# A seven-part change to the order of work in a one-core decoder-layer kernel: early input splits for the output GEMM, alternated squares, paired additions, earlier spreads, new cross-attention lanes

## The chip, the cores and the metric

One core of a Trainium2 chip runs the whole kernel. The metric is the device time of one execution in microseconds (us); lower is better. TensorE is called PE below, VectorE DVE, ScalarE ACT, GpSimd POOL and SyncE SP, as in the profile.

## The reference

One layer of a hybrid decoder, in float32, for a prompt of 512 tokens and a sample group of 8 x 4 tokens that share the weights (544 tokens in all, model width 1024):

```python
xn = rms_norm(x, lp['n_mix_pre'])
(m_qkv, s_z, s_xbc, s_dt, h_q, h_f, h_i, h_g, g_qkv, g_z, g_b, g_a) = split_cols(xn @ w_in, IN_SIZES)
# four mixers: block-sparse attention, Mamba-2 scan (ssm), HGRN2, gated DeltaNet (gdn)
# x = x + rms_norm(concat(o_a, o_b, o_c, o_d) @ w_out)
def memory_kv(mem, norm_w, w_kv):
    k, v = jnp.split(rms_norm(mem, norm_w) @ w_kv, 2, axis=-1)
def memory_cross_attention(xn, w_q, k, v, w_o):
    q = (xn @ w_q).reshape(b, L, X_HEADS, X_DH)
    s = jnp.einsum('blhd,bmhd->bhlm', q, k) * X_DH ** -0.5
    p = jax.nn.softmax(s, axis=-1)
    o = jnp.einsum('bhlm,bmhd->blhd', p, v)
    return o.reshape(b, L, X_HEADS * X_DH) @ w_o
def swiglu(xn, w_gu, w_down):
    g, u = jnp.split(xn @ w_gu, 2, axis=-1)
    return (jax.nn.silu(g) * u) @ w_down
```

Each of the three blocks has an RMS norm ahead of it and one behind it, and adds its result to x. Outputs are the new x, the new keys and values, the memory's keys and values, and the states.

## The kernel before

**Numbers and tiles.** Activations lie transposed, 128 channels on the partitions and 544 tokens along a row, as 8 tiles (KD = 8). Every large GEMM is done as three products: both operands are split into a high part in a short format and the rest as a low part, and PE adds high x high, high x low and low x high (`mm3`, `tile_mm`). A tile of 544 tokens is two halves of 272 (HT), each in its own PSUM bank, so one input tile k and one block of 128 output channels cost 6 matmuls of 272 columns. ACT makes the high part of a weight chunk (L239, `split_hi`) and POOL its low part (L248, `split_lo`); three chunks are in flight. The high parts of the inputs are made by ACT (`part_hi`, L743), the low ones by DVE (`part_lo`, a subtraction through `tt`, L706).

**Order.** Each engine has its program written out by hand; semaphores join them. A stage is a piece of each engine's program (`stage`). Where `enter` is true, an engine waits at its start until PE, DVE and ACT have all ended the stage before. Inside some stages several generators are interleaved by a string of letters, one letter for one step up to its next `yield`: `LANES` for the ssm stage ("m" the mixers, "p" the paged sample attention), `GDN_LANES` for the tail of the gated DeltaNet ("t") and the memory GEMM ("k"), `CX_LANES` for the cross stage ("p" prompt, "s" sample). All engines follow the same string.

**The ssm stage.** Two "p" steps come first (the sample's own scores, and the transposes of the first key tile into a bank), then the first "m" step: `spread_tensor` spreads two rows of per-head numbers over 128 partitions, four matmuls of 272 columns. DVE needs them for the inputs of the scan (`ssm_xdt`).

**The memory GEMM and the tail of gdn.** `mem_tensor` multiplies the memory with its 16 weight chunks, one "k" step each, then transposes the keys in four more steps. ACT splits a chunk in each step and copies two results in every second (L3112, L3119). Between them run the five token tiles of the gdn tail; the last step of a tile copies its outputs to OM tiles 6 and 7 (L3002), and its state update on DVE (two L706 additions and products ahead of that copy) is what PE needs for the next tile.

**The output GEMM (stage wout).** Its inputs are the 8 tiles of OM: 0 and 1 from attention, 2 and 3 from ssm, 4 and 5 from HGRN2, 6 and 7 from gdn. `wout_start_*` starts it: DVE squares tiles 6 and 7, PE sums the squares over heads (`sums`, matmuls with blk64, banks 6 and 7), ACT makes the roots (L976, L978), and DVE scales the tiles with them. Meanwhile PE does the products of tiles 0 to 5 for the first three output blocks (LAST = 3), then those of tiles 6 and 7. The first block's `gemm_mm` is what frees its weight slot.

**The norm transitions.** After the output GEMMs of the mixers (run 0) and of the cross attention (run 1), the sum over channels, the root, the residual and the next norm have to be done before the next GEMM's results can be scaled. It is done in two halves of tokens. DVE's `x_vector` makes the scaled tile (L936), the residual (L706) and the low part (L926) of each tile; ACT makes the high part (`x_hi_scalar`, L882) and the square (`x_square_scalar`, L886). PE starts the next GEMM on these parts (`next_start_tensor`). `pre_sum_vector` then adds the squares of the 8 tiles on DVE, PE sums them over partitions (`pre_sum_tensor`), ACT makes the root (L877, L878), and only then PE goes on.

**The cross stage.** A prompt step does the scores of one (head, token tile) pair on PE, the row maximum on DVE (L3191), the exponential on ACT (L3220), the scaling on DVE (L3197), the transposes on PE, and now and then a product with the values (pv). A sample step transposes one pair of memory key tiles and does one score; the first of these scores waits for queries that POOL pads (L3563 to L3569). Behind 16 sample scores come the sample softmax and eight products with values, whose loads go through four slots.

## Time and profile before

| | |
|---|---|
| median of 3 runs | 1240.22 us |
| lowest, highest | 1240.07, 1244.26 us |
| profiled execution: its own time | 1239.63 us |
| profiled execution: span | 1238.0 us |
| mean granted clock of TensorE | 0.969 |
| busy: PE, DVE, ACT, POOL | 94%, 48%, 36%, 36% |

The span is from the first to the last instruction; the time of an execution has some 1.6 us more around it. Busy shares are means over all stages. The granted clock is a share of 2.4 GHz; 0.50 is 1.2 GHz.

### The profile page before, as it was taken

How to read it: one execution, taken by the hardware profiler on the slowest of the kernel's cores; microseconds unless marked ns; L12 is line 12 of the kernel's file. 1: busy time of each engine (PE TensorE's matmuls, PEld its weight loads, DVE VectorE, ACT ScalarE, POOL GpSimd, SP SyncE). 2: the span in 40 equal slices, each digit the busy share in tenths (PEclk: the TensorE clock that was granted, in tenths of full speed). 3: DMA queues.
4: the chain of work that ended last, by engine and by line, in shares of the span. 5: the costliest groups of instructions: out<-in, count | busy, mean ns of one | idle time of the engine just before them, and what ended most of it. 6: DMA issues, size and time to landing. Idle time of an engine off the chain costs nothing.

```text
span 1238.0 us, 24845 instructions
## 1 busy us (share of the span) xinstructions
PE 1166.6 (94%) x10272; PEld 1014.0 (82%) x10272; DVE 598.7 (48%) x1068; ACT 448.9 (36%) x802; POOL 441.0 (36%) x370
## 2 busy tenths in 40 slices
PE   7999999988988988998989899999999999999998
PEld 6999997855655688887989656988999999977775
DVE  5699735236478886413291463184433334321003
ACT  6323234245544444233552342454222223221212
POOL 8433533053417121452603200614434444433331
PEclk9999999989979998898998899999999999999999
DMA  6332523066659422336414753312222232232221
GB/s 161 91 86 69 175 74 121 2 202 183 192 156 329 134 80 81 104 107 211 120 35 141 235 174 115 104 51 86 86 86 87 85 100 82 75 103 71 83 85 72
DMA packets 176581, 143.45 MB, mean 116 GB/s; under 512 B 15955, under 2 KB 162820, under 8 KB 176214
## 3 DMA queue, kind: packets, MB, share of 16 engines
q1 hardware_dynamic: 166838, 120.44, 32.5%
q0 software_dynamic: 7200, 20.23, 5.4%
q8 instruction: 81, 1.33, 0.5%
q10 hardware_dynamic: 2432, 1.21, 0.3%
q14 instruction: 30, 0.25, 0.1%
HBM read 131.64 MB, written 10.20 MB: 115 GB/s over the span
## 4 chain that ended last, share of the span: by engine, by line
PE 74%; DVE 12%; issue 4%; ACT 4%; POOL 2%; DMA 1%; SPq 1%; POOLq 0%; DVEq 0%; ACTq 0%
PE PS L264 67%; PE PS L267 7%; DVE SC L706 2%; DVE PROJ L1939 2%; POOL W_LO L248 2%; DVE XN L936 1%; DVE XT L706 1%; DVE PROJ L2358 1%; SPq L536 1%; DVE XN L706 1%; DVE XN_parts L926 1%; ACT PROJ L1342 1%; DVE PROJ L706 1%; ACT W_HI L239 0%; DVE PROJ L1940 0%
## 5 line engine op out<-in xcount | busy, mean ns | idle before, releaser
L248 POOL TENSOR_TENSOR W_LO<-W,W_HI 128x1024 fp32r<-128x1024 f32 x128 | 313.8, 2456 | 635.1 <-ACT W_HI L239 634.9
L264 PE MATMUL PS<-XN_parts,W_HI 128*128 128x272 f32 x1184 | 340.6, 288 | 0.0
L264 PE MATMUL PS<-OM_parts,W_HI 128*128 128x272 f32 x960 | 277.3, 289 | 0.0
L264 PEld LDWEIGHTS PS<-XN_parts,W_HI 128*128 128x128 f32 x1184 | 223.2, 188 | 0.0
L239 ACT ACTIVATE W_HI<-W 128x1024 fp32r<-128x1024 f32 x128 | 134.2, 1054 | 209.5 <-PE PS L264 209.5
L264 PE MATMUL PS<-OM_parts,W_LO 128*128 128x272 f32 x704 | 203.9, 290 | 0.0
L264 PE MATMUL PS<-SC_parts,W_HI 128*128 128x272 f32 x608 | 179.9, 296 | 3.9 <-POOL W_LO L248 3.2
L264 PEld LDWEIGHTS PS<-OM_parts,W_HI 128*128 128x128 f32 x960 | 181.8, 189 | 0.1
L264 PE MATMUL PS<-SC_parts,W_LO 128*128 128x272 f32 x608 | 176.8, 291 | 0.0
L264 PEld LDWEIGHTS PS<-OM_parts,W_LO 128*128 128x128 f32 x704 | 132.3, 188 | 0.0
L264 PEld LDWEIGHTS PS<-SC_parts,W_HI 128*128 128x128 f32 x608 | 115.6, 190 | 8.3 <-issue 6.1
L264 PEld LDWEIGHTS PS<-SC_parts,W_LO 128*128 128x128 f32 x608 | 115.4, 190 | 0.0
L264 PE MATMUL PS<-W_HI,PROJ_parts 128*128 128x512 f32 (+1 forms) x320 | 110.6, 374 | 0.0
L264 PE MATMUL PS<-W_HI,SC_parts 128*128 128x256 f32 (+1 forms) x288 | 87.3, 337 | 0.0
L264 PEld LDWEIGHTS PS<-W_HI,PROJ_parts 128*128 128x128 f32 x320 | 60.9, 190 | 13.3 <-issue 2.8
L706 DVE TENSOR_TENSOR SC<-SC 128x272 f32<-128x272 f32 (+6 forms) x68 | 37.2, 550 | 50.3 <-ACT SC L866 41.1
L264 PE MATMUL PS<-OM_parts,PROJ_parts 128*128 128x272 f32 x256 | 54.7, 303 | 5.9 <-DVE XN_parts L926 3.7
L264 PEld LDWEIGHTS PS<-W_HI,SC_parts 128*128 128x128 f32 x288 | 53.1, 197 | 8.4 <-issue 4.1
L264 PE MATMUL PS<-W_LO,SC_parts 128*128 128x512 f32 (+1 forms) x160 | 58.4, 365 | 0.0
L706 DVE TENSOR_TENSOR SC<-PS,RSQ 128x544 f32<-128x544 f32 x22 | 15.9, 724 | 87.1 <-PE PS L264 85.2
L3410 ACT ACTIVATE SC<-SC 128x544 f32<-128x544 f32 x22 | 14.5, 658 | 114.9 <-DVE SC L706 114.9
L1342 ACT ACTIVATE PROJ<-PS 128x512 f32<-128x512 f32 x68 | 40.1, 598 | 40.3 <-PE PS L267 40.3
(405 smaller groups left out, 2073.7 us busy)
## 6 DMA issues: line engine op xcount, KB each, us to landing
W<-in_w_gu SPq DMA_DIRECT2D x44, 512.0 KB, 3.9
W<-in_w_in SPq DMA_DIRECT2D x30, 512.0 KB, 3.8
W<-in_w_down SPq DMA_DIRECT2D x22, 512.0 KB, 3.7
W<-in_w_xkv SPq DMA_DIRECT2D x16, 512.0 KB, 3.7
W_scratch<-in_cache_moba_v SPq DMA_DIRECT2D x36, 128.0 KB, 4.8
W_scratch<-in_cache_moba_v POOLq DMA_DIRECT2D x36, 128.0 KB, 4.9
XT<-in_cache_moba_k SPq DMA_DIRECT2D x32, 128.0 KB, 2.8
XT<-in_cache_moba_k POOLq DMA_DIRECT2D x32, 128.0 KB, 2.4
```

What stands on the lines that cost most here:

```text
L239: nc.scalar.activation(hi_lo(n)[0], raw_chunk(n), ACT.Copy)\
L248: nc.gpsimd.tensor_tensor(hi_lo(n)[1], raw_chunk(n), hi_lo(n)[0].bitcast(F32), ALU.subtract).then_inc(S("weights_split"), 1)
L264: return nc.tensor.matmul(out, lhsT, rhs, start=start, stop=stop, skip_group_check=True)
L267: return nc.tensor.transpose(out, in_, ident[0:k, 0:k])
L536: sp.dma_start(dst, src).then_inc(S(name), 16)
L706: return V.tensor_tensor(out, x, y, op)
L926: V.scalar_tensor_tensor(lo(k)[:, TOKENS[run][j]], XT[:, k, TOKENS[run][j]], par(GAINS[run][1] + k), hi(k)[:, TOKENS[run][j]].bitcast(F32) ...
L936: last = V.scalar_tensor_tensor(xn[:, k, c_], xn[:, k, c_], par(GAINS[run][0] + k), rsq[:, c_], ALU.mult, ALU.mult)
L1342: return A.activation(o_, i_, ACT.Copy)
L1939: V.scalar_tensor_tensor(dst[:, d:SEQ], src[:, 0:SEQ - d], wt[3 - d], dst[:, d:SEQ], ALU.mult, ALU.add)
L2358: V.copy_predicated(h_store(i, w), level.bitcast(I32), src).then_inc(S("h_lv_out"), 1)
L3410: A.activation(f_g[:, t % 2, :], f_g[:, t % 2, :], ACT.Silu).then_inc(S("ff_silu"), 1)
```

## The change

Seven edits.

1. `ssm_start_tensor`: PE does the two spreads ahead of the lanes of the ssm stage.
2. `early_hi_scalar`, `early_lo_vector`: OM tiles 2, 3, 4, 0 and 1 are split during the memory GEMM, in ACT's "k" steps 10 to 14 and DVE's steps 11 to 15. Only tiles 5, 6 and 7 are split in stage wout.
3. `wout_start_tensor`: PE does the products of the five early tiles for block 0, then the first head sums, the five tiles of block 1, the second sums, block 2, then tile 5 and tiles 6 and 7 for all three blocks.
4. PE and DVE no longer wait at the entry of stage wout. In its place PE waits for the last copy of the gdn tail (`tail_vn_out`), and for the last copies of the memory's keys.
5. `y_gemm_scalar`: ACT makes a high part of the second half and then a square of the first half, tile by tile, and the squares of the second half at the end. Before it made all squares of the first half, then high part and square of the second half in turn.
6. `pre_sum_vector`: the squares of two tiles are added to two others at once (three additions of 2 x 272), then the two sums to each other.
7. `CX_LANES`: six prompt steps come right behind the first sample step; fewer are left at the end.

```diff
@@ -909,9 +909,9 @@
             for k in range(6, KD):
                 x_hi_scalar(s, run, 0, k)
             for k in range(KD):
+                x_hi_scalar(s, run, 1, k)
                 x_square_scalar(run, 0, k)
             for k in range(KD):
-                x_hi_scalar(s, run, 1, k)
                 x_square_scalar(run, 1, k)
             root_half_scalar(s, run, 3, 0)
             root_half_scalar(s, run, 4, 1)
@@ -942,32 +942,45 @@
             x_lo_vector(v, run, j, KD - 1)
+        EARLY = (2, 3, 4, 0, 1)
+
+        def early_hi_scalar(s, x):
+            s.wait_ge(*((S("states_made"), 3) if x < 3 else (S("tail_tok"), 5 + NT)))
+            A.activation(sc_hi[:, EARLY[x], :], OM[:, EARLY[x], :], ACT.Copy).then_inc(S("part_hi"), 1)
+
+        def early_lo_vector(v, x):
+            k = EARLY[x]
+            v.wait_ge(S("part_hi"), IN_BEFORE["wout"] + x + 1)
+            tt(OM_R[:, k, :], OM[:, k, :], sc_hi[:, k, :].bitcast(F32), ALU.subtract).then_inc(S("part_lo"), 1)
+
         def wout_start_tensor(pe):
             def sums(k):
                 for j in range(2):
                     last = mm(bank(6 + j)[:, 0:HT], blk64, half(g_qg[:, k, :], j), True, True)
                 last.then_inc(S("tail_sum"), 1)
+            def products(i, ks):
+                wh, wl = weights(pe, first["wout"] + i)
+                for k in ks:
+                    if i == 0:
+                        pe.wait_ge(S("part_lo"), IN_BEFORE["wout"] + (EARLY.index(k) if k in EARLY else k) + 1)
+                    for j in range(2):
+                        last = tile_mm(pe, half_bank("wout", i, j), "wout", wh, wl, TOKENS[0][j], [k], 0, EARLY[0], KD - 1)
+                return last
+
+            pe.wait_ge(S("tail_vn_out"), NT + 1)
+            products(0, EARLY)
+            pe.wait_ge(S("kvm_out"), 20)
             pe.wait_ge(S("tail_sq"), 3)
             sums(0)
+            products(1, EARLY)
+            pe.wait_ge(S("tail_root"), 6)
+            sums(1)
+            products(2, EARLY)
             for i in range(LAST):
-                wh, wl = weights(pe, first["wout"] + i)
-                for k in range(6):
-                    if i == 0:
-                        pe.wait_ge(S("part_lo"), IN_BEFORE["wout"] + k + 1)
-                    for j in range(2):
-                        tile_mm(pe, half_bank("wout", i, j), "wout", wh, wl, TOKENS[0][j], [k], 0, 0, KD - 1)
-                if i == 0:
-                    pe.wait_ge(S("tail_root"), 6)
-                    sums(1)
+                products(i, [5])
             for i in range(LAST):
-                wh, wl = weights(pe, first["wout"] + i)
-                for k in range(6, KD):
-                    if i == 0:
-                        pe.wait_ge(S("part_lo"), IN_BEFORE["wout"] + k + 1)
-                    for j in range(2):
-                        last = tile_mm(pe, half_bank("wout", i, j), "wout", wh, wl, TOKENS[0][j], [k], 0, 0, KD - 1)
-                last.then_inc(S("gemm_mm"), 1)
+                products(i, range(6, KD)).then_inc(S("gemm_mm"), 1)
             pe.wait_ge(S("tail_root"), 8)
         def wout_start_scalar(s):
@@ -977,11 +990,8 @@
                 s.wait_ge(S("tail_root"), 6 + 2 * k)
                 A.activation(g_qg[:, k, :], g_qg[:, k, :], ACT.Exp, scale=-0.5).then_inc(S("tail_root"), 1)
-            for k in range(3):
-                part_hi(s, "wout", k)
+            part_hi(s, "wout", 5)
             root(0)
-            for k in range(3, 6):
-                part_hi(s, "wout", k)
             root(1)
             for k in range(6, KD):
                 s.wait_ge(S("normed"), KD + k - 5)
@@ -994,8 +1004,7 @@
             v.wait_ge(S("tail_sq"), 3)
             for c_ in range(2):
                 link(V.scalar_tensor_tensor(Y[:, c_, :], Y[:, c_, :], par(R_GNORM), proj[:, C_GZ + c_, :], ALU.mult, ALU.mult))
-            for k in range(6):
-                part_lo(v, "wout", k)
+            part_lo(v, "wout", 5)
             for c_ in range(2):
                 v.wait_ge(S("tail_root"), 7 + 2 * c_)
                 tt(Y[:, c_, :], Y[:, c_, :], g_qg[:, c_, :], ALU.mult).then_inc(S("normed"), 1)
@@ -1032,12 +1041,10 @@
         def pre_sum_vector(v, run):
             for j in range(2):
                 c_ = TOKENS[run][j]
-                for k in range(1, KD):
-                    v.wait_ge(S("norm_sq_s"), 2 * KD * run + KD * j + k + 1)
-                    last = tt(nsq[:, 0, c_], nsq[:, 0, c_], nsq[:, k, c_], ALU.add)
-                    if k < KD - 1:
-                        link(last)
-                last.then_inc(S("pre_acc"), 1)
+                for k in range(2, KD, 2):
+                    v.wait_ge(S("norm_sq_s"), 2 * KD * run + KD * j + k + 2)
+                    link(tt(nsq[:, 0:2, c_], nsq[:, 0:2, c_], nsq[:, k:k + 2, c_], ALU.add))
+                tt(nsq[:, 0, c_], nsq[:, 0, c_], nsq[:, 1, c_], ALU.add).then_inc(S("pre_acc"), 1)
         KH = KF // 2
@@ -1968,6 +1975,11 @@
+        def ssm_start_tensor(pe):
+            pe.wait_ge(S("att_out"), 4)
+            for c_ in range(2):
+                spread_tensor(pe, 2 * c_, 0, c_)
+
         def ssm_tensor(pe):
             def pre(i):
                 t0, w, _ = TILES[i]
@@ -1986,9 +1998,6 @@
                     last = tr(bank(3)[0:w, k * P:(k + 1) * P], src, P)
                 last.then_inc(S("ssm_pre"), 1)
-            pe.wait_ge(S("att_out"), 4)
-            for c_ in range(2):
-                spread_tensor(pe, 2 * c_, 0, c_)
             yield
             pe.wait_ge(S("ssm_xdt"), 1)
             for i, (t0, w, _) in enumerate(TILES):
@@ -2999,7 +3008,12 @@
                 def outputs():
                     v.wait_ge(S("tail_o"), 5 + x + 1)
-                    link(V.tensor_copy(OM[:, 6:8, sl], bank(2)[:, 0:2 * w].rearrange("p (c l) -> p c l", l=w)))
+                    kept = V.tensor_copy(OM[:, 6:8, sl], bank(2)[:, 0:2 * w].rearrange("p (c l) -> p c l", l=w))
+                    if x < NT - 1:
+                        link(kept)
+                    else:
+                        kept.then_inc(S("tail_vn_out"), 1)
+                        v.wait_ge(S("tail_vn_out"), NT + 1)
                 if sample:
                     outputs()
@@ -3100,6 +3114,8 @@
                     gated = OM[:, 4 + step, :]
                     link(V.scalar_tensor_tensor(gated, gated, par(R_HNORM), proj[:, C_HG + step, :], ALU.mult, ALU.mult))
                     tt(gated, gated, h_norm[step], ALU.mult)
+                if 9 <= step < 14:
+                    early_lo_vector(v, step - 9)
                 yield
         def mem_scalar(s):
@@ -3111,6 +3127,8 @@
                         s.wait_ge(S("kvm_mm"), 2 * n + mt + 1)
                         A.activation(mkv[:, mt, n * 256:(n + 1) * 256], bank(MEM_BANKS[mt])[:, 0:256], ACT.Copy,
                                      scale=mem_rs[:, mt:mt + 1]).then_inc(S("kvm_out"), 1)
+                if 10 <= c_ < 15:
+                    early_hi_scalar(s, c_ - 10)
                 yield
             split_hi(s, first["wout"] + NH)
             for q in range(4):
@@ -3136,7 +3154,7 @@
         CX_Q = NPROJ // 2
         PV_STEP = (6, 8, 10, 12, 14, 16, 17, 18)
         CX_STEPS = 21
-        CX_LANES = "psps" * 8 + "psp" * 2 + "pps" + "psp" * 7 + "pspsppp"
+        CX_LANES = "ps" + "pppppp" + "psps" * 7 + "ps" + "psp" * 2 + "pps" + "psp" * 4 + "ps" * 5
         def cross_lanes(prompt, sample):
             steps = {"p": prompt, "s": sample}
@@ -3465,12 +3483,12 @@
         def _(pe):
             stage(pe, "inputs", lambda: inputs_tensor(pe))
             stage(pe, "win", lambda: normed_samples_tensor(pe), lambda: params_tensor(pe), lambda: win_tensor(pe), enter=False)
-            stage(pe, "ssm", lambda: lanes(mixer_lane(pe, ssm_tensor(pe), hgrn_tensor(pe)), moba_sample_tensor(pe), unit_tensor(pe), ssm_norm_tensor(pe)))
+            stage(pe, "ssm", lambda: ssm_start_tensor(pe), lambda: lanes(mixer_lane(pe, ssm_tensor(pe), hgrn_tensor(pe)), moba_sample_tensor(pe), unit_tensor(pe), ssm_norm_tensor(pe)))
             stage(pe, "gdn", lambda: gdn_tensor(pe), lambda: gdn_lanes(gdn_tail_tensor(pe), mem_tensor(pe)), enter=False)
             stage(pe, "wout",
                   lambda: wout_start_tensor(pe),
                   lambda: y_gemm_tensor(pe, "wout", LAST),
-                  lambda: wxq_tensor(pe))
+                  lambda: wxq_tensor(pe), enter=False)
             stage(pe, "cross", lambda: cross_lanes(cross_prompt_tensor(pe), cross_sample_tensor(pe)), enter=False)
             stage(pe, "wxo",
                   lambda: wxo_start_tensor(pe),
@@ -3489,7 +3507,7 @@
             stage(v, "wout",
                   lambda: wout_start_vector(v),
                   lambda: y_gemm_vector(v, "wout"),
-                  lambda: wxq_vector(v))
+                  lambda: wxq_vector(v), enter=False)
             stage(v, "cross", lambda: cross_lanes(cross_prompt_vector(v), cross_sample_vector(v)),
                   lambda: cross_out_vector(v), enter=False)
             stage(v, "wxo",
```

The order of PE's instructions where stage gdn ends and stage wout begins. `SC,XN` is the last product of the gdn tail, `CN,PROJ` the transposes of the memory's keys, `SC,CN` the head sums, and the rows with parts are products of the GEMM. Before:

```order
L264 MATMUL PS<-SC,XN 64x128 x4
L267 MATMUL PS<-CN,PROJ 128x128 x12
L264 MATMUL PS<-SC,CN 128x272 x2
L264 MATMUL PS<-SC_parts,W_HI 128x272
L264 MATMUL PS<-OM_parts,W_HI 128x272
```

With the change:

```order
L264 MATMUL PS<-SC,XN 64x128 x4
L267 MATMUL PS<-CN,PROJ 128x128 x12
L264 MATMUL PS<-SC_parts,W_HI 128x272
L264 MATMUL PS<-OM_parts,W_HI 128x272
L264 MATMUL PS<-SC_parts,W_LO 128x272
```

The sums went from ahead of the first product to behind the thirtieth.

ACT in the first norm transition, from the root of the first norm on (L877, L878). L882 is a high part, L886 a square. Before:

```order
L877 ACTIVATE RSQ<-PS,CN 128x272
L878 ACTIVATE RSQ<-RSQ 128x272
L882 ACTIVATE OM_parts<-XT,SM 128x272 x2
L886 ACTIVATE SC<-XT 128x272 x8
L882 ACTIVATE OM_parts<-XT,SM 128x272
L886 ACTIVATE SC<-XT 128x272
```

With the change:

```order
L877 ACTIVATE RSQ<-PS,CN 128x272
L878 ACTIVATE RSQ<-RSQ 128x272
L882 ACTIVATE OM_parts<-XT,SM 128x272 x3
L886 ACTIVATE SC<-XT 128x272
L882 ACTIVATE OM_parts<-XT,SM 128x272
L886 ACTIVATE SC<-XT 128x272
```

The eight squares in a row are gone from this place; at the end of the transition there are nine in a row instead.

PE at the start of the cross stage. `PROJ 128x256` are the scores of one prompt step, `CN,SC` its transposes, `CN,PROJ ... x8` one sample step's key transposes, `SC,XN` a sample score:

```order
 L264 MATMUL PS<-PROJ 128x256 x2
-L267 MATMUL PS<-CN,PROJ 128x128 x16
+L267 MATMUL PS<-CN,PROJ 128x128 x8
+L264 MATMUL PS<-PROJ 128x256 x2
+L267 MATMUL PS<-CN,SC 128x128 x2
+L264 MATMUL PS<-PROJ 128x256 x2
+L267 MATMUL PS<-CN,SC 128x128 x2
+L264 MATMUL PS<-PROJ 128x256 x2
+L267 MATMUL PS<-CN,SC 128x128 x2
+L267 MATMUL PS<-CN,PROJ 128x128 x8
 L264 MATMUL PS<-SC,XN 32x256 x4
```

Three prompt scores and three transposes now stand between the first sample step and the first sample score, which comes from behind two key tiles as before.

## Rows read from the trace of the kernel before

**Rows 1.** The page: busy time of PE, and the chain that ended last by engine
```profile
PE 1166.6 (94%) x10272; PEld 1014.0 (82%) x10272; DVE 598.7 (48%) x1068; ACT 448.9 (36%) x802; POOL 441.0 (36%) x370
...
PE 74%; DVE 12%; issue 4%; ACT 4%; POOL 2%; DMA 1%; SPq 1%; POOLq 0%; DVEq 0%; ACTq 0%
```

**Rows 2.** Windows of PE: from:to length, busy (instructions), granted clock, DMA share, GB/s
```profile
254.31:264.12 9.81, 9.81 (x49) 0.50 0.91 276
...
565.75:570.29 4.54, 1.71 (x4) 0.79 1.00 241
570.29:575.10 4.81, 4.81 (x21) 0.50 1.02 374
575.10:591.78 16.68, 16.68 (x129) 1.00 0.35 135
...
653.04:657.10 4.06, 4.06 (x18) 0.50 0.01 4
816.00:839.23 23.23, 18.15 (x132) 1.00 0.00 1
...
693.59:698.00 4.41, 4.41 (x20) 0.50 1.13 316
```

**Rows 3.** Timeline, ssm start: start, length, engine, instruction [idle before <- releaser]; last row the chain
```profile
253.24 0.60 PE L264 MATMUL PS<-SC 128*128 128x32 f32 x4 [3.41 <-DVE W L1688]
256.25 1.11 ACT L2291 ACTIVATE W<-W 128x1088 f32<-128x1088 f32 x1
260.79 0.66 PE L264 MATMUL PS<-PROJ,W 128*32 128x128 f32 x8
...
254.31 3.87 PE PS L264 x8
```

**Rows 4.** Timeline of PE where stage wout begins
```profile
565.09 0.66 PE L267 MATMUL PS<-CN,PROJ 128*128 128x128 f32 x4 [0.25 <-ACT PROJ L3119]
...
567.89 1.71 PE L264 MATMUL PS<-SC,CN 128*128 128x272 f32 x4 [2.14 <-DVE SC L706]
570.29 0.57 PE L264 MATMUL PS<-SC_parts,W_HI 128*128 128x272 f32 x1 [0.69 <-DVE OM_parts L706]
```

**Rows 5.** Groups of 566 to 592: the input parts (xcount, busy us, mean ns)
```profile
L743 ACT ACTIVATE SC_parts<-OM 128x544 fp32r<-128x544 f32 x8 | 4.8, 646 | 0.4 <-DVE OM L706 0.2
L706 DVE TENSOR_TENSOR OM_parts<-OM,SC_parts 128x544 fp32r<-128x544 f32 x8 | 5.4, 720 | 0.3 <-ACT SC_parts L743 0.2
```

**Rows 6.** Timeline of the memory GEMM, and of DVE at 592
```profile
548.75 0.66 DVE L706 TENSOR_TENSOR XN<-XN,SM 128x128 f32<-128x128 f32 x1 [0.55 <-PE PS L264]
552.84 0.47 ACT L3112 ACTIVATE PROJ<-PS,SM 128x256 f32<-128x256 f32 x1 [0.96 <-PE PS L264]
...
592.00 4.81 DVE L706 TENSOR_TENSOR SC<-SC 128x544 f32<-128x544 f32 x2 [10.18 <-ACT SC L866]
```

**Rows 7.** Timeline of the first norm transition, and one double addition at 607
```profile
607.14 0.73 DVE L706 TENSOR_TENSOR SC<-SC 128x544 f32<-128x544 f32 x1 [5.33 <-ACT SC L866]
...
635.26 0.50 DVE L926 SCALAR_TENSOR_TENSOR XN_parts<-XT,SM,OM_parts 128x272 fp32r<-128x272 f32 x1 [0.70 <-ACT OM_parts L882]
644.17 6.50 DVE L706 TENSOR_TENSOR SC<-SC 128x272 f32<-128x272 f32 x14
650.73 1.28 PE L264 MATMUL PS<-SC,CN 128*128 128x272 f32 x2 [1.74 <-DVE SC L706]
653.04 0.60 PE L264 MATMUL PS<-OM_parts,PROJ_parts 128*128 128x272 f32 x1 [1.04 <-ACT RSQ L878]
```

**Rows 8.** Timeline of the cross stage
```profile
688.28 2.49 DVE L3197 TENSOR_SCALAR SC<-SC 128x256 f32<-128x256 f32 x1
693.59 0.66 PE L264 MATMUL PS<-SC,XN 128*32 128x256 f32 x4 [5.30 <-POOL XN L3569]
734.68 0.35 DVE L3197 TENSOR_SCALAR SC<-SC 128x256 f32<-128x256 f32 x1
735.09 0.44 PE L267 MATMUL PS<-CN,SC 128*128 128x128 f32 x2 [0.97 <-DVE SC L3197]
```

## The prediction

> **What bounds the kernel now.** I read the chain of waits first. TensorE (PE) is 94% of the span busy and holds 74% of the chain, DVE 12% [rows 1]: nearly everything that counts is either PE working or PE waiting for one short chain elsewhere. So a change can win only where PE stands still, or where it works at the low clock. The windows view shows the second kind [rows 2]: at a granted clock of 0.50, that is 1.2 of 2.4 GHz, PE worked for 9.81 us after 254.31, 4.81 us after 570.29, 4.06 us after 653.04 and 4.41 us after 693.59. Each of these follows a stretch in which PE stood still or nearly so; 816.00 to 839.23 has as much idle time (5.1 us of 23.2) at a clock of 1.00, so whether a gap is followed by the low level differs from gap to gap. The four stretches come to 23.1 us, of which half is lost. The diff touches just those places: the ssm start, the start of the output GEMM, both norm transitions, and the start of the cross stage. Outside them the order of work is the same, and there PE is dense: I assume that what is won passes through to the end.
>
> **Part 1, the ssm start.** PE waits 3.41 us for DVE before 253.24 [rows 3], and right behind, from 254.31, runs the four spread matmuls for 3.87 us at the low level. Now the spreads come first. They need only the stage entry (about 250.8) and the attention outputs, so at 2.4 GHz they take about 1.9 us and end by 252.8, inside the idle stretch. What is late next is ScalarE: it copies the second key transpose only after a table load and the activation that ends at 257.36 [rows 3]; with a 0.6 us copy the second score can start at 258.0 where it started at 260.79. That is 2.8 us. If PE is also at 2.4 GHz there, the next 3.3 us of work take half, and it is 4.6 us. PE now idles some 2 us at 256, so I take 3.4 us, between the two; from below the bound is 0, if a wait further on in this stage swallows it.
>
> **Part 2, the start of the output GEMM.** Before, PE ends the memory transposes at 565.75, waits 2.14 us for the squares that DVE starts after the stage barrier, does the head sums, waits 0.69 us for the first low part, and starts the products at 570.29 [rows 4], the first 4.81 us of them at 0.50 [rows 2]. Now five of eight tiles are split beforehand, DVE does not wait for the barrier, and PE starts products of those five at once: at 566.0, counting 0.25 us for the last drain. Idle time won: 2.14 + 0.69 - 0.25 = 2.6 us. The low clock: PE has no gap any more between 565.75 and 570.29, so I expect the 6.1 us of work between 568.3 and 575.1 at full rate, 3.0 us. Sum 5.6 us. Nothing is late next: 30 products at 0.125 us (16.68 us for 129 instructions, sums among them [rows 2]) take 3.8 us, so the first sums run at 569.8, the second at 574.4; the roots, the gating of tiles 6 and 7 and their two parts (0.65 and 0.72 us a tile [rows 5]) are done by 579, and PE asks for tile 6 at 581. The last 36 products, during which the next weights are made, keep their order, so the 1.7 us wait for those weights stays. Bounds: 2.6 us if the clock falls anyway, 5.9 us if the drain costs nothing.
>
> The five splits themselves lie on ScalarE and DVE during the memory GEMM, where both idle. Ten instructions of 0.65 or 0.72 us; two of ScalarE's delay a weight split by 0.6 us; PE waited for no weights between 500 and 590, so there is cover. One place is tight: ScalarE makes the fourth high part after its copy at 552.84 [rows 6], so at 553.95; DVE stands waiting for it with the state update behind it that before ran at 548.75, and PE asks for that state at 555.60. 553.95 + 0.72 + 0.66 + 0.29, with gaps, is 555.7: about 0.1 us late. The row that speaks against it: two DVE additions of the same size took 4.81 us together, 2.4 each, at 592.00 [rows 6] while POOL made low parts of weights. If the fourth split takes 2.4 us, PE waits 1.8 us. In the Trainium skill, GPSIMD Engine Reference, Key points, POOL shares its SBUF interfaces with DVE, and contention is stated for DVE instructions with two SBUF inputs; these splits are of that kind. By that rule the sum would be 1.8 us smaller. The trace agrees at 592.00; I keep 0.1 because before POOL's next W_LO starts at 554.33, and the ScalarE split ahead of it moves back 0.65 us, behind most of this one.
>
> **Part 3, the two norm transitions.** ScalarE did eight squares of the first half in one run before the second half's first high part, and DVE waited 0.70 us for that part (635.26 [rows 7]). With high part and square alternating, ScalarE needs 0.9 us a tile and DVE 1.3 us, so high parts come as soon as the residual is there: 0.70 us won. Then the 14 additions took 6.50 us. Now they are 6 of double width at 0.73 us plus a semaphore gap (607.14 [rows 7]) and 2 single ones at 0.46: 6 x 0.77 + 2 x 0.46 = 5.5 us, 1.0 us less. The last square of the second half is ready at 646.0, before it is needed. The sum of the second half is ready 1.7 us earlier, PE's sum at 650.73 moves with it, and so does the restart at 653.04, behind two ScalarE instructions. The second transition has the same rows (14 additions in 6.50 us, the same waits). 2 x 1.7 = 3.4 us. That the clock does not fall at the first would add 2.4 us (0.56 of the 1.28 us sum, half of 4.06 us less the drop's end); that it falls at the second, where it did not before, would take as much away. I put this at nothing.
>
> **Part 4, the cross stage.** Three more prompt steps come ahead of the first sample score, which waits 5.30 us for POOL's padded queries [rows 8]. They fill part of the gap, not all: the first of them needs DVE's scaling, which is held until 690.77 beside POOL's work (2.49 us against 0.35 elsewhere), so PE still idles about 2.4 us from 688.3. From there PE does four scores and three transposes where it did one and two key tiles, but at 1.20 GHz if the clock falls as before at 691.4: about as much time lost as won. At the other end fewer prompt steps are left to cover the sample softmax; the wait of 0.97 us at 735.09 [rows 8] becomes one of 1 to 2 us. Net 0, between -2 us (clock low and longer waits) and +2.5 us (clock stays up).
>
> **Sum.** 3.4 + 5.6 + 3.4 + 0 = 12.4 us off the profiled execution's 1239.6 us: 1227.2 us. The median of the three runs is 0.6 us above that execution, so I predict 1227.8 us.
>
> **Rivals.**
> The clock does not come back. Gaps remain everywhere (2 us at 256, 1.3 us before the second norm sum, 2.4 us at 688). Then parts 1 and 2 give 2.8 and 2.6, part 3 gives 3.4 and part 4 takes 2: 6.8 us, 1233.4 us. For it: the low level came after four of five such gaps. Against: behind 565.75 no gap is left. In the Trainium skill, TensorE: Matmul & The Clock Gate, Part 1, the default state is throttled and activity releases it; the rows agree, and do not say how much idle time is enough. Chance 0.18.
> The ssm start is absorbed and the cross stage loses. The 3 us go into waits for ScalarE's copies or the page loads between 258 and 350, and part 4 costs 2 us: 5.6 + 3.4 - 2 = 7.0 us, 1233.2 us. For it: ScalarE, not PE, ends the waits of that stage. Against: they are few. Chance 0.15.
> POOL stretches the early splits as priced above: 1.8 us less, 1229.6 us. Chance 0.04.
> Slower than before: the low clock spreads. The cross stage now begins with PE waiting on DVE and ScalarE at every step, and the GDN tail has one wait more. A low stretch costs half its length, 2.0 us (653.04) to 4.9 us (254.31). From six short or three long new ones on, the 12.4 us are gone; with eight short ones, 16 us, it is 1243.8 us. Against it: total idle time falls. Chance 0.03.
> The forecast has the remaining 0.60.
>
> **How the numbers follow.** All good ends together (4.6, 5.9, 5.8 and 2.5) give 18.8 us, 1221.4 us; the two middle rivals lie at 1233, and with a little more lost at 1236. Range 1220 to 1236. A measurement of this kernel tells about 0.5%, 6.2 us, from no change: faster means under 1234.0. The forecast lies there nearly whole, the rivals at 1233 a little over half: faster 0.82, same 0.15, slower 0.03.
>
> **What would show it.** Right: the four spread matmuls before PE's wait at the ssm start, and the second score 3 to 4 us earlier; less than 0.5 us between the last memory transpose and the first product, at a clock of 1.00; 14 additions replaced by 8 in 5.5 us; restarts of both transitions 1.7 us earlier relative to their GEMM; the cross stage as long as before. Wrong: a PE wait over 1 us in the GDN tail for DVE's state, a wait for tile 6 at the output GEMM, a span of the ssm stage that does not shrink, or a cross stage longer by more than 2 us.

## The result, and the profile after

The changed kernel took 1226.6 us (median of 4 executions, 1225.0 to 1230.0), against 1240.6 us for the kernel before on the same chip (median of 4, 1240.1 to 1244.3): a ratio of 0.988, with a 95% interval of 0.985 to 0.991. That is 14 us faster; 1227.8 us was forecast, with a range of 1220 to 1236. The profiled execution took 1227.1 us at a span of 1225.5 us, 12.5 us below the profiled span of before.

The page of the changed kernel, busy times and chain by engine:

```profile
PE 1159.9 (95%) x10272; PEld 1008.6 (82%) x10272; DVE 597.9 (49%) x1056; ACT 448.6 (37%) x802; POOL 441.8 (36%) x370
...
PE 74%; DVE 13%; issue 4%; ACT 3%; POOL 2%; DMA 1%; SPq 1%; POOLq 0%; DVEq 0%; ACTq 0%
```

Nothing of the picture has changed against [rows 1]: PE bounds it. PE's busy time is 6.7 us lower with the same 10272 instructions, and the mean granted clock is 0.976 where it was 0.969. I read those 6.7 us as work that ran at 2.4 GHz where it ran at 1.2, and the rest as idle time; the table below, stretch by stretch, has 8.5 us less of low clock, part of which PE sat through idle. The same windows of PE as in [rows 2], at their new places (from:to length, busy (instructions), granted clock, DMA share, GB/s):

```profile
254.22:264.00 9.78, 8.67 (x83) 0.83 0.89 269
366.09:370.65 4.56, 4.56 (x36) 0.63 0.88 255
402.66:408.75 6.09, 6.09 (x102) 0.56 0.78 256
564.02:568.00 3.98, 3.98 (x31) 1.00 1.01 247
568.00:584.23 16.23, 16.23 (x123) 1.00 0.69 254
642.82:647.22 4.40, 4.40 (x23) 0.61 0.02 4
826.71:831.00 4.29, 4.29 (x34) 1.00 0.00 0
677.77:680.42 2.65, 0.00 (x2) 1.00 0.81 249
680.42:684.77 4.35, 4.35 (x16) 0.61 1.15 308
```

The start of the output GEMM (564.02) is at full clock now. The ssm start is mostly so. Behind the first transition (642.82) and at the cross start (680.42) a low stretch is still there, though shorter. And there are two low stretches where before had none or a shorter one, at 366 and at 403.

The ssm start and the start of stage wout on PE, which answer to [rows 3, 4]:

```profile
251.31 2.10 PE L264 MATMUL PS<-OM,CN 4*128 4x272 f32 x8 [0.87 <-DVEq L3463]
253.75 0.63 PE L264 MATMUL PS<-SC 128*128 128x32 f32 x4 [0.35 <-DVE W L1695]
...
258.68 0.42 PE L264 MATMUL PS<-PROJ,W 128*32 128x128 f32 x8 [1.11 <-ACT PROJ L1349]
...
563.10 0.66 PE L267 MATMUL PS<-CN,PROJ 128*128 128x128 f32 x4 [0.25 <-ACT PROJ L3137]
564.02 0.36 PE L264 MATMUL PS<-SC_parts,W_HI 128*128 128x272 f32 x1 [0.26 <-issue]
...
567.88 1.08 PE L264 MATMUL PS<-SC,CN 128*128 128x272 f32 x4
```

The spreads (8 records, 2.10 us) fill the wait of 3.41 us down to 0.35. At 564.02 the first product follows the last transposes after 0.26 us, and the sums at 567.88 wait for nothing.

Both transitions, DVE and PE, which answer to [rows 7]:

```profile
635.66 5.34 DVE L706 TENSOR_TENSOR SC<-SC 128x544 f32<-128x544 f32 x8
638.43 0.73 PE L264 MATMUL PS<-SC,CN 128*128 128x272 f32 x2 [0.22 <-DVE SC L706]
641.06 0.73 PE L264 MATMUL PS<-SC,CN 128*128 128x272 f32 x2 [1.15 <-DVE SC L706]
642.82 0.40 PE L264 MATMUL PS<-OM_parts,PROJ_parts 128*128 128x272 f32 x1 [1.04 <-ACT RSQ L878]
...
824.95 0.72 PE L264 MATMUL PS<-SC,CN 128*128 128x272 f32 x2 [1.15 <-DVE SC L706]
826.71 0.39 PE L264 MATMUL PS<-OM_parts,PROJ_parts 128*128 128x272 f32 x1 [1.04 <-ACT RSQ L878]
```

Eight additions take 5.34 us where fourteen took 6.50, and PE's wait for the last sum is 1.15 us where it was 1.74.

**Where the 12.5 us went.** The same instruction was looked up in both traces at the borders of each stretch, and the difference of the starts taken. "Low" is what the clock costs in it: one minus the granted clock, summed over the stretch in pieces of 0.25 us of the windows view, in us. Where PE stands still during a low piece it costs less than that.

| stretch of PE, by the start in the trace of before | before, us (low) | after, us (low) |
|---|---|---|
| ssm start, 248.91 to 264.76 | 15.85 (5.1) | 11.49 (1.7) |
| mixers, first part, 264.76 to 369.03 | 104.27 (10.2) | 104.15 (10.2) |
| mixers, second part, to 444.49 | 75.46 (3.4) | 78.73 (6.8) |
| gdn to 519.91 | 75.42 (6.8) | 74.04 (5.1) |
| gdn tail and memory GEMM to 563.75 | 43.84 (0) | 43.83 (0) |
| start of the output GEMM to 591.49 | 27.74 (3.4) | 22.18 (0) |
| output GEMM to 626.60 | 35.11 (0) | 34.94 (0) |
| first transition to 653.04 | 26.44 (1.5) | 23.94 (0) |
| its restart to 657.84 | 4.80 (1.9) | 4.52 (1.7) |
| cross, first part, 671.04 to 700.03 | 28.99 (3.4) | 29.33 (1.7) |
| cross, second part, to 761.24 | 61.21 (0) | 61.04 (0) |
| second transition, 799.97 to 839.58 | 39.61 (0) | 37.41 (0) |

Beside these only the start of the program moved (0.6 us later, a load). The gain of 4.4 us at the ssm start is paid back by 3.3 us in the second part of the mixers, and there the low column accounts for all of it (3.4 us).

### The profile page after: what moved, and what is told of

Its sections match the earlier page's. It is cut to its first block, busy times and chain, and to the rows that moved or that the text cites. A ratio compares the mean times of both kernels' runs of the same rounds, so it can differ in the third digit from the quotient of the medians.

```text
span 1225.5 us, 24818 instructions
## 1 busy us (share of the span) xinstructions
PE 1159.9 (95%) x10272; PEld 1008.6 (82%) x10272; DVE 597.9 (49%) x1056; ACT 448.6 (37%) x802; POOL 441.8 (36%) x370
## 4 chain that ended last, share of the span: by engine, by line
PE 74%; DVE 13%; issue 4%; ACT 3%; POOL 2%; DMA 1%; SPq 1%; POOLq 0%; DVEq 0%; ACTq 0%
PE PS L264 67%; PE PS L267 7%; DVE SC L706 2%; DVE PROJ L1946 1%; POOL W_LO L248 1%; DVE XN L936 1%; DVE XT L706 1%; DVE PROJ L2367 1%; SPq L536 1%; DVE XN L706 1%; DVE XN_parts L926 1%; ACT PROJ L1349 1%; DVE PROJ L1947 1%; DMA XN<-in_cache_mem_v 1%; DVE PROJ L706 1%
## 5 line engine op out<-in xcount | busy, mean ns | idle before, releaser
L706 DVE TENSOR_TENSOR SC<-SC 128x544 f32<-128x544 f32 (+7 forms) x56 | 35.3, 633 | 46.9 <-ACT SC L866 38.0
```

The source lines that it names most:

```text
L706: return V.tensor_tensor(out, x, y, op)
```

## The experiments

Twelve kernels ran, in four groups; in each group the kernel before ran beside them. Ratios are to it, with their 95% interval. Executions of one kernel scatter by 3 to 14 us, so a ratio resolves some 3 us, and the stretches of the trace are what tells the parts apart.

| kernel | median, us | ratio to before |
|---|---|---|
| edit 1 alone | 1239.7 | 0.998 (0.996 to 1.001) |
| edits 2, 3, 4 alone | 1235.3 | 0.995 (0.992 to 0.997) |
| edits 5, 6 alone | 1235.4 | 0.995 (0.993 to 0.997) |
| edit 7 alone | 1242.3 | 1.000 (0.998 to 1.002) |
| the changed kernel again | 1226.1 | 0.990 (0.987 to 0.993) |
| changed, old lanes | 1228.8 | 0.991 (0.988 to 0.994) |
| changed, sums first | 1230.7 | 0.991 (0.988 to 0.994) |
| changed, sums repeated | 1227.3 | 0.989 (0.986 to 0.991) |
| changed, zero fills late | 1226.7 | 0.988 (0.985 to 0.991) |
| changed, sums first, entry waits | 1230.0 | 0.990 (0.989 to 0.992) |
| edit 6 alone | 1237.7 | 0.996 (0.994 to 0.997) |
| changed, fills late and sums repeated | 1224.5 | 0.986 (0.983 to 0.989) |

Kernel before in the four groups: 1241.8, 1241.9, 1242.6 and 1241.5 us. The four parts alone give -2.1, -6.5, -6.3 and +0.6 us by their medians, -14.3 in all, as the whole change does (-14.0); each of the four is known to some 3 us only, so the close agreement is luck.

**The ssm start alone.** The kernel before, with edit 1:

```diff
+            pe.wait_ge(S("att_out"), 4)
+            for c_ in range(2):
+                spread_tensor(pe, 2 * c_, 0, c_)
...
-            pe.wait_ge(S("att_out"), 4)
-            for c_ in range(2):
-                spread_tensor(pe, 2 * c_, 0, c_)
             yield
```

> The kernel before with edit 1 alone (the spreads ahead of the lanes of the ssm stage). The forecast's step gives 3.4 us. In the changed kernel the shift of PE was 4.4 us behind the ssm start, but only some 2.6 us of it were left at 520. Theory A (the gain is real at its place, and further on it is eaten by low stretches of PE at 367 to 371 and 401 to 409, which come with the new timing): 2.0 to 4.4 us faster, the second score near 258.1 to 258.7, and whatever is missing behind 300 is in longer low stretches. Theory B (a wait for DVE or ACT between 270 and 480 swallows it): under 1 us faster, with new or longer waits in the mixers, and the low stretches as before.

The ssm start took 13.77 us with 5.1 of low, against 15.85 us with the same 5.1 before: 2.1 us. Behind it nothing was lost (104.28, 75.47 and 75.47 us with the same low as before). Timeline of PE, and the window over it:

```profile
249.91 2.51 PE L264 MATMUL PS<-OM,CN 4*128 4x272 f32 x8 [0.87 <-DVEq L3447]
252.35 1.06 PE L264 MATMUL PS<-SC 128*128 128x32 f32 x4
...
257.91 0.65 PE L264 MATMUL PS<-PROJ,W 128*32 128x128 f32 x8 [1.11 <-ACT PROJ L1342]
```

```profile
252.35:261.89 9.54, 8.43 (x53) 0.51 0.87 276
```

The order is as in the changed kernel, but here PE is at 1.2 GHz until 261.89. So theory A holds at its lower end, by the trace; the ratio of the medians (0.996 to 1.001) can't be told from no change. The edit itself is worth 2.1 us, and the other 2.3 us of the changed kernel's 4.4 are a clock that was up.

**The start of the output GEMM alone.** The kernel before, with edits 2 to 4 (their diff stands above).

> The kernel before with edits 2, 3 and 4 alone (early splits, new order of the output GEMM's start, no entry wait). Theory A (idle time won 2.6 us and a low stretch of 6.1 us of work at full rate, 3.0 us): 5.6 us faster, no row at a clock of 0.50 between 563 and 590, and PE reaches the last product of the first three blocks 5.6 us earlier than before. Theory B (part of the 5.6 us seen there in the changed kernel comes from the shifted time at which it arrives, that is, from edit 1): 2.6 to 4 us faster, with a low stretch behind 566 again.

The stretch took 22.17 us with no low time, 5.6 us less than before. Theory A. It was 22.17 or 22.18 us in all seven profiles with these edits, and with the old start 27.74, 27.70, 27.73 and 27.69 us with 3.4 of low (the kernel before, and with edit 1, edits 5 and 6, edit 7 alone) and 27.07 us with 1.7 (edit 6 alone). Of the five low stretches this is the only one that goes with the edit each time.

**Both transitions alone**, edits 5 and 6; and **edit 6 alone**.

> The kernel before with edits 5 and 6 alone (squares alternated with high parts, additions in pairs). Forecast: 1.7 us at each transition, 3.4 us in all. The changed kernel showed 2.5 and 2.0 us, 4.5 in all. Theory A (1.7 us of waits each time; the rest of the first transition is a low stretch at 643 that happened to be shorter): 3.4 to 4.5 us faster. Theory B (PE loses at the second transition, where the clock stays up before, one low stretch): 1 to 2 us faster with a granted clock of 0.50 behind the second restart.

> The kernel before with edit 6 alone (additions in pairs). Theory A (additions and alternation each win their own wait, as the kernel with both showed 1.95 us at each transition: 0.8 at the residuals, 1.17 at the sums): each transition 1.1 to 1.2 us shorter by unchanged clock, about 2.3 us in all, and DVE's wait of 0.70 us for the second half's first high part still there. Theory B (the pairs only help because the alternation brings the squares in time): under 0.5 us at each transition, and a new wait of DVE for ACT's squares.

With both, the first transition took 23.94 us. Of the kernels that keep the old code, those without low time in it took 25.88 and 25.89: 1.95 us won. The second: 37.41 against 39.39 and 39.34, 1.95 us again, and 2.2 against the 39.61 of the kernel before, which has no low time there either. With the pairs alone they took 24.73 and 38.63 us: 1.15 us won at the first, 0.75 at the second, with 0.4 of low in it. DVE in the first transition with the pairs alone:

```profile
637.67 0.50 DVE L926 SCALAR_TENSOR_TENSOR XN_parts<-XT,SM,OM_parts 128x272 fp32r<-128x272 f32 x1 [0.70 <-ACT OM_parts L882]
...
646.58 4.11 DVE L706 TENSOR_TENSOR SC<-SC 128x544 f32<-128x544 f32 x6
```

The wait of 0.70 us is still there, as theory A of the second text says, and the additions run through. So the pairs give 1.15 and the alternation 0.8 us. In the kernel with both, a low stretch came up behind the second restart and cost 1.7 us, as theory B of the first text has it; the kernel with edit 7 alone, which keeps the old transitions, has one there too, of 2.7 us. The won waits are theory A's; the clock sits on top of them, with or without the edit. The median was 6.3 us lower (3.6 to 8.6 by the interval of the ratio), more than either theory said; the interval holds theory A's 3.4 to 4.5 us in part and excludes theory B's 1 to 2.

**The cross lanes alone, and the changed kernel with the old ones.**

> The kernel before with edit 7 alone (the new lanes of the cross stage). Theory A (what is won in front of the first sample score is lost in the waits at the other end): between 0.5 us faster and 0.5 us slower, with a wait of PE near 688 of 2 to 3 us in place of 5.30, and waits of 1.5 to 2.6 us for the sample softmax. Theory B (the new lanes are worth something by themselves, and in the changed kernel the clock took it away): 1.5 us faster or more. Theory C (they cost, and the clock hid it): 1.5 us slower or more.

> The changed kernel with the old CX_LANES. Theory A (edit 7 is worth nothing, 0.2 us in the trace of the kernel with edit 7 alone): within 1 us of the changed kernel, the cross stage as long as before (from the restart of the first transition to the start of the cross output GEMM). Theory B (the lanes gain once the stage comes earlier): 2 us slower than the changed kernel. Theory C (they cost): 1.5 us faster than it.

The first part of the cross stage took 29.39 us (1.7 low) with the new lanes alone, 29.26 (3.4 low) in the changed kernel with the old ones; over all kernels the new lanes gave 29.33 to 29.56 with 1.7 of low, the old ones 28.78 to 29.26 with 3.4. So they do halve the low stretch each time. It is worth less than 1.7 us: in the kernel before PE stood idle in 2.4 of its 6.8 us (691.2 to 693.6), so it cost 2.2 us, and 1.7 with the new lanes. Against that PE's idle time in both parts together went from 6.4 to 7.2 us in the changed kernel. The second part is about as long (61.0 to 61.4 us, 61.9 once, against 61.2). Theory A: worth nothing, or 0.2 to 0.5 us on the wrong side. The medians (1242.3 against 1241.8, 1226.1 against 1228.8) go either way. The second pair, 2.7 us apart, is what theory B of the second text named, but the intervals of the two kernels overlap, and no stretch of the cross stage shows it.

**The changed kernel again.**

> The changed kernel itself, again, so that the next three kernels have it beside them, and to see how far its executions scatter and with what. Theory A (executions of one kernel differ by how much of the span PE works at the low clock): the times follow the mean granted clock, some 0.9 to 1.0 us for each 0.001 of it, as in the 33 runs of the kernel before (1235.7 to 1249.4 us). Theory B: they scatter with no relation to it. In either case a median of 1225 to 1230 us.

Theory A. Of six executions four had a mean granted clock of 0.975 or 0.976 and took 1225.1 to 1226.2 us; the other two had 0.969 and 0.967 and took 1232.0 and 1234.3. In the profiled one the low stretches lay elsewhere than in the first profile of the same kernel:

```profile
641.30:645.70 4.40, 4.40 (x36) 1.00 0.03 9
824.00:829.00 5.00, 4.96 (x27) 0.66 0.06 17
366.39:369.31 2.92, 2.92 (x37) 1.00 1.02 308
```

At the restart of the first transition the clock is 1.00 where it was 0.61, and at that of the second it is 0.66 where it was 1.00, with the same gaps of 1.15 and 1.04 us in front. The extra low stretch at 366 is not there, and the second part of the mixers took 75.51 us, as before. The kernel with edit 6 alone, whose order of work is the old one up to there, took 79.70 us with 6.8 of low in the same part. So the 3.3 us that the first profile lost there need no cause in the change.

**Sums first, and then the entry waits too.** The changed kernel, with the first head sums ahead of the products of block 0; in the second kernel PE and DVE also wait at the entry of stage wout again.

```diff
             pe.wait_ge(S("tail_vn_out"), NT + 1)
-            products(0, EARLY)
             pe.wait_ge(S("kvm_out"), 20)
             pe.wait_ge(S("tail_sq"), 3)
             sums(0)
+            products(0, EARLY)
```

> The changed kernel with the first head sums ahead of the first block's products again, as before, all else kept (the splits are still made early). PE then waits for DVE's squares, some 2.1 us less what the missing entry barrier gives. Theory A (the 3.0 us of the clock hang on this gap): the gap comes back, a low stretch of 4 to 5 us follows, and it is 4 to 5 us slower than the changed kernel. Theory B (the clock came back because of the timing, not because the gap is gone): only 1.5 to 2.2 us slower, with a clock of 1.00 behind the sums.

> As the changed kernel with the first sums ahead (where PE's gap came out at 0.73 us, since DVE no longer waited for the entry), and with the entry waits of stage wout back on PE and DVE. The early splits stay. Theory A (the low stretch of 6.8 us behind 568 in the kernel before follows from a gap of some 2.1 us there): the gap of about 2.1 us is back, a low stretch follows, and this part is 3 to 5 us longer than in the changed kernel. Theory B (the low stretch came from the whole weak minute before, two gaps of 2.14 and 0.69 us and the wait for the low part): gap of 2.1 us, clock 1.00 behind it, 1.6 to 2.1 us longer.

Start of the output GEMM, with the sums first:

```profile
564.99 0.66 PE L267 MATMUL PS<-CN,PROJ 128*128 128x128 f32 x4 [0.25 <-ACT PROJ L3137]
566.38 1.15 PE L264 MATMUL PS<-SC,CN 128*128 128x272 f32 x4 [0.73 <-ACT PROJ L3137]
```

```profile
566.38:570.38 4.00, 4.00 (x28) 1.00 0.99 220
```

With the entry waits too, DVE and PE, and the windows of PE:

```profile
561.66 0.66 PE L267 MATMUL PS<-CN,PROJ 128*128 128x128 f32 x4 [0.25 <-ACT PROJ L3137]
563.01 1.29 DVE L706 TENSOR_TENSOR SC<-OM 128x1088 f32<-128x1088 f32 x1 [2.09 <-ACTq L3463]
564.45 1.05 PE L264 MATMUL PS<-SC,CN 128*128 128x272 f32 x2 [2.14 <-DVE SC L706]
```

```profile
564.45:568.90 4.45, 4.45 (x19) 0.62 1.04 291
568.90:580.00 11.10, 11.10 (x87) 1.00 0.76 297
```

In the first kernel the gap I had expected at some 2.1 us was 0.73: DVE no longer stands at the entry, its squares start right behind its last copy, and PE now waits only for ACT's last copy. No low stretch followed, and the stretch took 22.65 us, 0.5 more than in the changed kernel; both theories had the gap wrong, so it tells nothing between them. Its median is 4.5 us above the changed kernel's, as theory A said, but not by this place: of the 5.2 us between the two profiles 3.3 lie ahead of 249 us and 1.3 at the ssm start. In the second the gap is 2.14 us, as in [rows 4], a low stretch follows at once, and the stretch takes 25.67 us, 3.5 more. Of that 1.7 are clock. This is theory A, with its price. All 14 profiles agree: the six with the gap of 2.14 us in front of the sums (the kernel before, edit 1, edits 5 and 6, edit 6, edit 7, and this one) have a low stretch within 3 us of its end, the eight without the gap have none up to the end of the stretch. The three kernels also cut part 2 into its pieces: from 27.7 us the early splits lead to 25.67, the missing entry waits to 22.65, and the new order of the sums to 22.18. That is 2.0, 3.0 and 0.5 us, of which 1.7 in each of the first two are clock. The 1.7 of the first piece are not shown to be the splits': with edit 6 alone, which keeps the old start, the low stretch there was also short (1.7), and the stretch took 27.07 us.

**PE kept busy in the gaps of the transitions.** The changed kernel, with

```diff
+                            if i == 2:
+                                mm(bank(1)[:, 0:HT], ones, nsq[:, 0, TOKENS[run][0]], True, True)
                             if i > 0:
                                 pre_sum_tensor(pe, run, i - 1)
+            pe.wait_ge(S("norm_root"), 4 + 4 * run + 3)
+            mm(bank(0)[:, 0:HT], ones, nsq[:, 0, TOKENS[run][0]], True, True)
```

> The changed kernel with PE kept busy in the two gaps of each norm transition: one matmul over 272 tokens (0.73 us) repeated in front of the last sum (a gap of 1.15 us in the changed kernel) and one behind it (a gap of 1.04 us), both into banks that nobody reads then. Theory A (the low stretch of 643 to 647, 2 us of loss, follows from these gaps): no row at 0.50 behind the first restart, 1 to 2 us faster. Theory B (whether PE falls to the low level there is settled by other things, or by gaps further back): the low stretch stays, and the time is the same or up to 0.6 us worse by the added matmuls.

```profile
644.32:648.50 4.18, 4.18 (x33) 1.00 0.02 4
```

No low stretch at either restart, and the transitions were as long as without it (23.94 and 37.55 us). But the unaltered kernel had none at the first restart either in its second profile, nor had two later kernels that leave the transitions as they are (fills late, and sums first with the entry waits). PE's gaps in front of the last sum and of the restart went from 1.15 and 1.04 us to 0.69 and 0.58. The medians are 1227.3 and 1226.1 us. With one profile each this doesn't decide; it only shows that the repeats cost nothing.

**POOL's zero fills held back.** The changed kernel, with

```diff
             g.wait_ge(S("gemm_mm"), GEMM_MM["wxq"] + KD)
+            g.wait_ge(S("att_probs"), 16 + 1)
             link(G.memset(cx_qp, 0.0), "g")
```

> The changed kernel, with POOL holding its two zero fills of the cross stage (1.81 and 0.55 us) until DVE has scaled the first prompt step. Theory A (the fill beside it is what makes that scaling last 2.48 us instead of 0.35, and PE's gap of 2.65 us comes from it): the first scaling takes 0.35 us, PE's first gap falls to about 0.5 us, the second scaling, which now meets the fills, is the long one, and from the first score to the sixth sample step 1 to 1.5 us are won; the padded queries come some 0.2 us later and nobody waits for them. Theory B (that scaling is long for another reason, such as being the first of the stage, or POOL's last low parts): it stays at 2.4 us, and the time does not change.

In the changed kernel, POOL, DVE and PE at the start of the cross stage:

```profile
676.03 2.35 POOL L248 TENSOR_TENSOR W_LO<-W,W_HI 128x1024 fp32r<-128x1024 f32 x1 [3.64 <-ACT W_HI L239]
677.79 2.48 DVE L3215 TENSOR_SCALAR SC<-SC 128x256 f32<-128x256 f32 x1
678.32 1.81 POOL L3581 MEMSET XN<- 128x2048 f32 x1
680.42 0.41 PE L267 MATMUL PS<-CN,SC 128*128 128x128 f32 x2 [2.65 <-DVE SC L3215]
```

With the fills held back:

```profile
673.00 2.35 POOL L248 TENSOR_TENSOR W_LO<-W,W_HI 128x1024 fp32r<-128x1024 f32 x1 [3.64 <-ACT W_HI L239]
674.75 0.74 DVE L3215 TENSOR_SCALAR SC<-SC 128x256 f32<-128x256 f32 x1
675.62 1.80 POOL L3582 MEMSET XN<- 128x2048 f32 x1 [0.27 <-DVE SC L3215]
675.64 0.41 PE L267 MATMUL PS<-CN,SC 128*128 128x128 f32 x2 [0.91 <-DVE SC L3215]
676.85 0.72 DVE L3215 TENSOR_SCALAR SC<-SC 128x256 f32<-128x256 f32 x1
...
678.92 0.35 DVE L3215 TENSOR_SCALAR SC<-SC 128x256 f32<-128x256 f32 x1
```

Theory A in its cause, with other numbers. In the changed kernel the scaling ends at 680.27, just behind the end of the fill (680.13): it began beside the low part, and the fill followed that without a break. Held back, the first scaling ends at 675.49, behind the end of the low part (675.35), and the second at 677.57, behind that of the fill (677.42). Each costs 0.4 us and not 2.1. PE's gap of 2.65 us becomes three of 0.91, 0.71 and 0.39, the clock stays at 1.00, and the first part of the cross stage takes 27.36 us, 2.0 less, of which 1.7 are the low stretch that is gone. That the second scaling would be the long one, as theory A had it, did not come true. The median did not show it (1226.7 us): in this profile low stretches came up at 745 and at 824.

**Both of the last two.**

> The changed kernel with both of the last two edits: POOL's zero fills held until the first scaling, and one matmul repeated in each gap of the norm transitions. In their profiles the first stretch of the cross stage was 2.0 to 2.1 us shorter (0.4 us of idle time, 1.7 us of a low stretch that was gone), and neither transition had a low stretch behind its restart. Theory A (both hold here as well): the cross stage's first stretch 2 us shorter than in the changed kernel, no low stretch at either restart, and 2 to 3 us faster in all, 1223 to 1225 us. Theory B (a low stretch that goes in one place comes up in another; what counts is the sum over the whole span): those places as in A, but low stretches elsewhere, and a median within 1 us of the changed kernel's 1226.

The cross stage's first part took 27.37 us again and its second 59.99 (1.0 less than in the changed kernel; 0.9 of it is that PE waited 0.81 us for a load of values where it waited 1.69, which neither edit aims at), no restart had a low stretch, and the median was 1224.5 us, against 1226.1 and 1226.6 for the changed kernel. Theory A, though the intervals (0.983 to 0.989 against 0.987 to 0.993) overlap: the fastest kernel of this study, by some 2 us that are not quite shown.

## Why the prediction was right, point by point

**Part 1, the ssm start, 3.4 us.** The spreads went into the wait, and ScalarE's second key copy was late next, as written. The second score started 8.24 us behind the last product of the stage before (258.68 less 250.44), where it was 10.95 (260.79 less 249.84): 2.7 us, for 2.8 forecast. The clock was then up and made it 4.4. But in the kernel with this edit alone it was not, and the edit gave 2.1 us; in the nine profiles with it the stretch lasted 11.5 to 13.9 us with 1.7 to 5.1 of low. The term was right for this execution and a little high as a mean (1.9 to 4.4 us won, 2.8 in the middle one of the nine). The step that was off is the bound of 2.8 us for a low clock: it took the spreads at 2.4 GHz, and where they and the first transposes run at the low level too, 2.1 us are left. The rival of an absorbed gain is not borne out as a rule. In the profile it seems so (3.3 us lost again between 369 and 444), but the second profile of the same kernel doesn't have it. In one of the nine the gain did go: with the sums repeated the low stretch ran on into the mixers, whose first part took 106.81 us where it takes 104.27, and only 0.3 us were left of both together.

**Part 2, the output GEMM, 5.6 us.** It gave 5.56 us, as 2.6 of idle time and 3.0 of clock, within the bounds of 2.6 and 5.9, and in each kernel that had it. The early splits cost nothing. The state update ran at 552.54, 3.8 us later than before, behind the split for which DVE had waited 3.74 us, and still in time: the memory GEMM and gdn tail took 43.83 us, as before. The rival that POOL stretches these splits did occur, in the third of them (2.03 us) and, less, in the fifth (1.04), where nobody was waiting, and took nothing. The fourth, for which it was priced, ended at 552.62, before POOL's next low part:

```profile
538.00 2.86 POOL L248 TENSOR_TENSOR W_LO<-W,W_HI 128x1024 fp32r<-128x1024 f32 x1 [0.18 <-ACT W_HI L239]
542.90 4.67 POOL L248 TENSOR_TENSOR W_LO<-W,W_HI 128x1024 fp32r<-128x1024 f32 x2 [2.04 <-ACT W_HI L239]
546.13 2.03 DVE L706 TENSOR_TENSOR OM_parts<-OM,SC_parts 128x544 fp32r<-128x544 f32 x1
551.90 0.73 DVE L706 TENSOR_TENSOR OM_parts<-OM,SC_parts 128x544 fp32r<-128x544 f32 x1 [3.74 <-ACT SC_parts L949]
552.54 0.28 DVE L706 TENSOR_TENSOR XN<-XN,SM 128x128 f32<-128x128 f32 x1
552.89 5.22 POOL L248 TENSOR_TENSOR W_LO<-W,W_HI 128x1024 fp32r<-128x1024 f32 x2 [5.32 <-ACT W_HI L239]
554.83 1.04 DVE L706 TENSOR_TENSOR OM_parts<-OM,SC_parts 128x544 fp32r<-128x544 f32 x1
```

The third took 2.03 us and the same instruction later 0.73. In the Trainium skill, GPSIMD Engine Reference, Key points, contention with POOL is stated for DVE instructions that read two inputs from SBUF; by it these splits can be held, and the trace agrees with its 2.03 us. The page names a second kind, DVE instructions in a two-port performance mode; the scaling of the cross stage reads one tile and a column and was held too (2.48 us against 0.35), and whether it is of that kind no run here shows.

**Part 3, the transitions, 3.4 us.** They gave 1.95 us each at an even clock (2.2 at the second by the kernel before itself), for 1.7 forecast: 0.8 for the 0.70 us wait, and 1.15 for additions that took 5.34 us where 5.5 was expected. The rest of the 2.5 us at the first is 0.5 us of low time that lay over the last sum before. The clock at the restarts was put at nothing. That was right on the mean only, as far as the profiles tell: at both restarts together the clock costs 0 to 6.8 us (2.7 on the mean) in the five kernels without the alternation, and 0 to 3.4 us (1.9) in the seven with both edits and no repeats. Which of the two restarts has it differs between executions of one kernel.

**Part 4, the cross stage, 0.** It lost 0.3 us in its first part and won 0.2 in its second. PE's gap came to 2.65 us, for 2.4 forecast, from the scaling beside POOL. The new waits at the end are 1.7 us for a scaling on DVE, 1.1 us for the sample's probabilities, and 1.7 us for a load of values: 4.5 us, where the forecast had one of 1 to 2 us in place of 0.97. That term was too small by at least 2.5 us. The part with them is not longer, since three of its prompt scores and their transposes now lie in the first part. The forecast put the net at 0 without adding these terms up, so the near zero is in part luck.

**The sum.** 12.5 us in the profile for 12.4 forecast. The agreement to 0.1 us is luck. Part 1 gave 1.0 us more than forecast and part 3, with its restart, 1.6 us; 1.4 us came between 444 and 520, all of it clock. Against them stand 3.3 us lost between 369 and 444, clock again, and 0.6 us at the start of the program. The measured difference of the medians is 14.0 us; the profiled executions' is 12.5. The rival that the low clock spreads had nothing for it: the mean granted clock went from 0.969 to 0.976. How much is won without the clock can be estimated from the group in which the changed kernel ran again: a line through the 11 executions of the kernel before gives 1239.8 us at a clock of 0.969 and 1241.4 at 0.967, and the changed kernel took 1232.0 and 1234.3 us there. So some 7 to 8 us are idle time that is gone, as the traces have it (2.1 at the ssm start, 2.6 at the output GEMM, 3.9 in the transitions, less 0.8 in the cross stage, 7.8 in all); the rest comes with the clock. The rival that it doesn't come back holds for the ssm start of the kernel with edit 1 alone, not for part 2.

## What to carry to other kernels

Price a gap of the bounding engine twice: once for its length and once for the clock that may fall behind it, and take the second as a chance unless the gap goes away altogether; of five places only one lost its low stretch entirely in every run. When a wait is removed by reordering, ask whether it was the order or an entry barrier of the engine behind it that made it: here the barrier held the largest piece, 3.0 of 5.6 us. And to read a change of 1% in a program whose executions scatter by as much, compare the same stretch over several kernels' traces, not the spans.

## What the runs showed of the hardware

A DVE instruction that meets a running POOL instruction can be held until that one ends: a TENSOR_SCALAR of 128x256 took 0.35 us alone, 0.72 to 0.74 when POOL's ended 0.6 us after its start, and 2.48 us over a low part and the fill behind it, each time ending 0.14 to 0.15 us after POOL. A MEMSET, which reads no tile, holds it as a subtraction does. The subtraction of 128x544 on DVE (0.73 us alone) took 2.03 and 1.04 us beside POOL's and ended 0.58 us after it.

Whether a held instruction gets in between two of POOL's differs. The scaling did not get in between the low part (to 678.38) and the fill behind it (from 678.32). The subtraction at 554.83 did, between two low parts (to 555.29, from 555.25); the second of them then took 2.87 us where it takes 2.35. In the same way the low part that began at 538.00, 0.12 us after the start of a split, took 2.86 us. So DVE delays POOL too. What decides who goes first these runs do not show.

Not every DVE instruction is held: beside the low part from 676.03 on a copy of 128x512 out of PSUM took 0.69 us and a reduction of 128x256 out of PSUM 0.42, as elsewhere, and beside POOL's copies of 128x16 (0.20 us each) the scaling took 0.35 us.

Executions of one kernel differ chiefly in how long TensorE runs at its low level. Over the 33 executions of the kernel before in the first group the span falls by 0.9 us for each 0.001 of mean granted clock (a fitted line), and the times go from 1235.7 to 1249.4 us. With gaps of 1.15 and 1.04 us in front, one restart was found at 0.61 and at 1.00 in two executions of the same kernel. What decides between them stays open.
